# Differential attention in layers 0 and 3: six tiles of queries and keys by Strassen's scheme

## The reference, cut to what matters

```python
def diff_attention(h, w_in, lam, subln_g, w_out, rel_bias, lam_init):
    q, k, v = jnp.split(h @ w_in, 3, axis=-1)
    q = q.reshape(B, S, DA_HEADS, 2, HEAD_DIM)
    k = k.reshape(B, S, DA_HEADS, 2, HEAD_DIM)
    v = v.reshape(B, S, DA_HEADS, 2 * HEAD_DIM)
    ...
        s = jnp.einsum('bqhcd,bkhcd->bhcqk', qb, k).astype(jnp.float32) * scale + bias[None]
        pr = masked_softmax(s, mask)
        a = pr[:, :, 0] - lam_full * pr[:, :, 1]
        return jnp.einsum('bhqk,bkhe->bqhe', a.astype(v.dtype), v)
    ...
    o = rmsnorm(o, subln_g) * (1.0 - lam_init)
    return o.reshape(B, S, D_MODEL) @ w_out
```

## Time and profile before

| | us |
|---|---|
| median of 3 runs | 2436.51 (2435.25 to 2438.89) |
| the profiled execution | 2434.99 |
| its span in the trace | 2433.0 |

### The profile page before, as it was taken

How to read it: one execution, slowest core, us unless ns; L and a number is a source line. 1 busy time by engine, 2 the same in 40 slices (tenths; PEclk the granted TensorE clock), 3 DMA queues, 4 the chain that set the end, 5 groups by cost and what they waited for, 6 DMA issues and landing times.

```text
span 2433.0 us, 31769 instructions
## 1 busy us (share of the span) xinstructions
PE 2338.7 (96%) x12496; PEld 1549.0 (64%) x12496; DVE 1033.6 (42%) x2557; ACT 562.3 (23%) x1350; POOL 89.4 (4%) x125
## 2 busy tenths in 40 slices
PE   7999999999999999999999999999999989999997
PEld 5689648768945777964787974767433348743333
DVE  1447764455676333766532867623200017220001
ACT  2333003342301322210323320223111122311111
POOL 1000000000000000000000000100000000000000
PEclk9999999999999999999999999999999999999999
DMA  9435754413765332666432575642999995289996
GB/s 364 184 139 213 282 197 173 148 61 130 265 255 208 130 121 104 237 248 242 152 125 104 200 279 212 234 176 90 384 377 387 393 357 198 100 350 421 394 393 260
DMA packets 67347, 564.97 MB, mean 232 GB/s; under 512 B 7162, under 2 KB 9523, under 8 KB 19587
## 3 DMA queue, kind: packets, MB, share of 16 engines
q1 hardware_dynamic: 47232, 470.60, 50.4%
q0 software_dynamic: 15696, 83.24, 8.9%
q10 hardware_dynamic: 4274, 9.12, 1.0%
HBM read 688.72 MB, written 26.45 MB: 294 GB/s over the span
## 4 chain that ended last, share of the span: by engine, by line
PE 64%; DMA 8%; DVE 3%; ACT 2%; issue 1%; POOL 0%; SPq 0%; POOLq 0%; ACTq 0%; DVEq 0%
PE work L501 51%; PE acc L501 12%; DMA weight_ring<-in_stream 5%; DMA expert_rows<-oT 1%; PE work L555 1%; DMA bias<-in_stream 1%; DVE oT L2185 1%; PE acc L555 1%; DMA big<-expert_rows,row_index 0%; DMA token_rows<-big,token_slot 0%; DMA hT<-token_rows 0%; DVE xT L2220 0%; ACT big L1655 0%; SPq L3050 0%; DVE big L2198 0%
## 5 line engine op out<-in xcount | busy, mean ns | idle before, releaser
L501 PE MATMUL work<-hT,weight_ring 128*128 128x256 f32 (+1 forms) x1984 | 387.0, 354 | 3.5 <-DVE stat_max L2371 2.5
L501 PEld LDWEIGHTS work<-hT,weight_ring 128*128 128x128 f32 x1984 | 338.5, 191 | 45.4 <-issue 6.3
L501 PE MATMUL work<-weight_ring,big 128*64 128x512 f32 (+2 forms) x1344 | 293.3, 585 | 12.4 <-DMA weight_ring<-in_stream 7.1
L501 PE MATMUL work<-oT,weight_ring 128*128 128x256 f32 (+1 forms) x1280 | 245.5, 349 | 0.0
L501 PEld LDWEIGHTS work<-oT,weight_ring 128*128 128x128 f32 x1280 | 214.1, 191 | 24.3 <-issue 2.0
L2937 DVE TENSOR_TENSOR big<-work,big 128x512 f32<-128x512 f32 x16 | 11.1, 692 | 472.5 <-PE work L501 472.5
L501 PEld LDWEIGHTS work<-weight_ring,big 128*64 128x64 f32 (+2 forms) x1344 | 89.2, 128 | 179.3 <-issue 176.9
L501 PE MATMUL work<-weight_ring,att 128*32 128x512 f32 (+2 forms) x640 | 174.1, 597 | 4.1 <-ACT att L1655 4.1
L1655 ACT ACTIVATE big<-work 128x512 f32<-128x512 f32 x121 | 69.4, 596 | 321.8 <-PE work L501 297.2
L501 PE MATMUL work<-hT,att 128*128 128x128 f32 (+1 forms) x960 | 141.2, 296 | 0.0
L501 PE MATMUL work<-weight_ring,hT 128*128 128x512 f32 x288 | 129.8, 602 | 11.8 <-DMA weight_ring<-in_stream 10.7
(11 more groups left out here) (366 smaller groups left out, 3032.7 us busy)
## 6 DMA issues: line engine op xcount, KB each, us to landing
weight_ring<-in_stream SPq DMA_DIRECT2D x120, 2048.0 KB
weight_ring<-in_stream SPq DMA_DIRECT2D x226, 1024.0 KB, 8.4
ada_ring<-in_stream SPq DMA_DIRECT2D x56, 1024.0 KB
bias<-in_stream SPq DMA_DIRECT2D x56, 1024.0 KB
ada_ring<-in_ada_stream POOLq DMA_DIRECT2D x48, 1024.0 KB, 7.3
expert_rows<-oT POOLq DMA_DIRECT2D x20, 512.0 KB, 9.3
hT<-token_rows ACTq DMA_DIRECT2D x18, 512.0 KB
token_rows<-bias POOLq DMA_DIRECT2D x11, 512.0 KB, 12.7
```

Of the source, the lines that this page charges most:

```text
L501: return pe.matmul(o, a, b, start=start, stop=stop, skip_group_check=True)
```

## The change

Six of the eight tiles of queries and keys, f = 2 and 3 in layer 0 and f = 0 to 3 in layer 3, are computed by Strassen's scheme in the variant with seven products (Winograd's sums). The weights of a tile are split in queries and keys and in the first and second half of the 1024 inputs; h is split by halves of inputs and halves of tokens. A product is 2 x 4 matmuls of 128 x 128 (16 records), so a tile has 56 matmuls of 128 columns instead of 32 of 256.

Products 1, 6, 7 and 4 accumulate in one PSUM bank (the chain): ACT copies the bank after product 1 (`act_mixed`) and product 5's bank; DVE adds after product 6 (L2505, then product 7 may start) and after product 7 (L2515, then product 4 may start). Product 2 is added by L2499, product 3 by L2526; then L2527 multiplies the late keys by `rstd` in place, L2529 scales all queries, and L2531 multiplies the chain bank, after product 4, into the early keys, which frees the bank.

GpSimd makes four weight sums per tile, 128x1024 each (L3178), in `ada_ring`, and four input sums per layer, 128x512 each (L3183 to L3188). There is one set of slots: a tile's sums 1, 2, 3, 4 wait until products 5, 6, 7, 3 of the tile before are done. The loads of the adaptive weights come behind them on GpSimd's queue: the first pair behind layer 0's sums, one pair behind layer 3's.

In layer 3 tiles 0 and 1 run their seven products in one go, in the order 1, 5, 6, 2, 7, 3, 4; all others as 2, 1, 5, 6 in one step and 7, 3, 4 in the next. In layer 3 the mean over squares of step 4 moves behind the fill (`late_mean`).

The diff, cut to its core:

```diff
+        def mixed(st):
+            return range(2 if first_da(st) else 0, 4)
+        def together(st, f):
+            return not first_da(st) and f < 2
+        def mixed_order(st, f):
+            return (1, 5, 6, 2, 7, 3, 4) if together(st, f) else (2, 1, 5, 6, 7, 3, 4)
+        def mixed_banks(st, f):
+            parts = units_of(st)[0]
+            chain, third = parts[2 + 2 * f], parts[3 + 2 * f]
+            fifth, second = (chain - 1, chain + 1) if together(st, f) else (chain - 1, chain - 2)
+            return {1: chain, 6: chain, 7: chain, 4: chain, 2: second, 5: fifth, 3: third}
+        def pe_mixed(pe, st, p):
...
+            for at, product in enumerate(order[begins:begins + 4], begins):
+                o, w, data = operands[product]
+                if product in (1, 2, 3, 5):
+                    pe_open(pe, banks[product])
+                if product in (3, 5, 6, 7):
+                    pe.wait_ge(head_weights, 4 * g + {5: 1, 6: 2, 7: 3, 3: 4}[product])
+                if product in (4, 5, 6, 7):
+                    pe.wait_ge(head_inputs, 4 * (st.layer > 0) + {5: 1, 6: 2, 7: 3, 4: 4}[product])
+                if product == 6:
+                    pe.wait_ge(chain_kept, g + 1)
+                elif product in (7, 4):
+                    pe.wait_ge(chain_added, 2 * g + (1 if product == 7 else 2))
+                for m in range(2):
+                    for k in range(4):
+                        ins = mm(pe, o[:, m * P:m * P + P], w[:, k, m * P:m * P + P], data[:, k],
+                                 (m, k) == (0, 0) and product in (1, 2, 3, 5), k == 3)
...
                 for p in fill_of(st)[s]:
-                    pe_part(pe, st, p, parts[p])
+                    if is_mixed(st, p):
+                        pe_mixed(pe, st, p)
+                    else:
+                        pe_part(pe, st, p, parts[p])
+                if late_mean(st, s):
+                    sub_squares(0)
...
+        def act_mixed(act, st, p):
+            wait_mixed(act, st, f, 1)
+            nc.scalar.activation(q_early, wk(banks[1], 0, S).rearrange("p (m t) -> p m t", m=2), ACT.Copy).then_inc(chain_kept, 1)
+            wait_mixed(act, st, f, 5)
+            nc.scalar.activation(k_late, wk(banks[5], 0, S).rearrange("p (m t) -> p m t", m=2),
+                                 ACT.Copy).then_inc(evac[banks[5] % 4], 1)
...
+        def dve_mixed_heads(v, st, p):
+            wait_mixed(v, st, f, 3)
+            v.wait_ge(chain_added, 2 * g + 2)
+            v.tensor_tensor(q[:, :, P:S], third, q[:, :, P:S], ALU.add).then_inc(evac[banks[3] % 4], 1)
+            v.tensor_tensor(k[:, :, P:S], k[:, :, P:S], by(1), ALU.mult)
+            wait_evacuated(v, [banks[2], banks[3]])
+            v.scalar_tensor_tensor(q, q, DH ** -0.5, over_tokens(2), ALU.mult, ALU.mult)
+            wait_mixed(v, st, f, 4)
+            v.tensor_tensor(k[:, :, 0:P], chain, by(0), ALU.mult).then_inc(evac[banks[4] % 4], 1)
...
+        def pool_mixed(pool, st):
+            def weights(f):
+                pool.wait_ge(landed[tile.slot], 16 * tile.turn)
+                for i, product, a, b, op in ((1, 5, w(1, 0), w(1, 1), ALU.add), (2, 6, mixed_weight_sum(1), w(0, 0), ALU.subtract),
+                                             (3, 7, w(0, 0), w(1, 0), ALU.subtract), (4, 3, w(0, 1), mixed_weight_sum(2), ALU.subtract)):
+                    if f > mixed(st)[0]:
+                        wait_mixed(pool, st, f - 1, product)
+                    if i in (2, 4):
+                        pool.wait_ge(head_weights, n + i // 2)
+                    pool.tensor_tensor(mixed_weight_sum(i), a, b, op).then_inc(head_weights, 1)
+            weights(mixed(st)[0])
+            pool.wait_ge(h_ready, 8 * st.at["h"])
+            pool.wait_ge(work_full, units_of(st)[2]["means"] + 1)
...
+            for f in mixed(st)[1:]:
+                weights(f)
+            wait_mixed(pool, st, 3, 3)
...
             copy_rows(pool, rows2, copies2, 0, 8, copies_out[2])
+            first_mixed, second_mixed = [st for st in plan if st.kind == "da"]
+            pool_mixed(pool, first_mixed)
             for a in range(2):
                 pool.dma_start(ada_ring[:, a, :], ada_stream[a]).then_inc(ada_landed[a], 16)
...
                 pool_gate_sums(pool, ple)
+                if ple.layer + 1 == second_mixed.layer:
+                    pool.wait_ge(ada_step, 16 * (end + 1))
+                    pool_mixed(pool, second_mixed)
+                    for a in range(2):
+                        pool.dma_start(ada_ring[:, a, :], ada_stream[2 * end + 2 + a]).then_inc(ada_landed[a], 16)
```

More of the change, by code:

```diff
@@ L620, in nsa_done, with late_mean @@
             return [p[0] if isinstance(p, tuple) else p for p in NSA_FILL.get(s, ()) if not isinstance(p, tuple) or p[1] == 1]
+        def late_mean(st, s):
+            return s == 4 and st.kind == "da" and not first_da(st)
         def units_of(st):
@@ L636, in units_of @@
                 at += 1
+                if kind == "da" and not first_da(st) and p == 2:
+                    parts[p] = at
+                    at += 2
                 if kind == "fox" and p == 1:
@@ L657, in units_of @@
                     at += 2
-                if kind == "da" and s in (4, 6):
+                if kind == "da" and s in (4, 6) and not late_mean(st, s):
                     other[(s - 4) // 2] = at
@@ new lines, in is_mixed, with wait_mixed, mixed_weights @@
+        def is_mixed(st, p):
+            return st.kind == "da" and 2 <= p < 10 and p // 2 - 1 in mixed(st)
+        def wait_mixed(eng, st, f, product):
+            if product in (1, 7, 4):
+                eng.wait_ge(head_products, 3 * mixed_number(st, f) + (1, 7, 4).index(product) + 1)
+            else:
+                eng.wait_ge(work_full, mixed_banks(st, f)[product] + 1)
+        def mixed_weights(st, f, upper, later):
+            whole_tile = slot_of(tiles[st.at["tile"] + 1 + f].slot, 0, TILE).rearrange("p (k c) -> p k c", k=KB)
+            return whole_tile[:, 4 * later:4 * later + 4, upper * S:upper * S + S]
@@ new lines, in mixed_weight_sum, with mixed_input, mixed_input_sum @@
+        def mixed_weight_sum(i):
+            return slot_of(RING, (i - 1) * 1024, 1024).rearrange("p (k c) -> p k c", k=4)
+        def mixed_input(later, late):
+            return hT[:, :].rearrange("p (k c) -> p k c", k=KB)[:, 4 * later:4 * later + 4, late * P:late * P + P]
+        def mixed_input_sum(i):
+            return blk(big, SQ + 2 * (i - 1), 2).rearrange("p (k c) -> p k c", k=4)
+        def pe_mixed(pe, st, p):
+            f, g = p // 2 - 1, mixed_number(st, p // 2 - 1)
+            banks, order, begins = mixed_banks(st, f), mixed_order(st, f), 4 * (p % 2)
+            second, fifth, chain, third = (wk(banks[n], 0, S) for n in (2, 5, 1, 3))
+            weights = lambda upper, later: mixed_weights(st, f, upper, later)
+            operands = {1: (chain, weights(0, 0), mixed_input(0, 0)), 2: (second, weights(0, 1), mixed_input(1, 0)),
+                        3: (third, mixed_weight_sum(4), mixed_input(1, 1)), 4: (chain, weights(1, 1), mixed_input_sum(4)),
+                        5: (fifth, mixed_weight_sum(1), mixed_input_sum(1)), 6: (chain, mixed_weight_sum(2), mixed_input_sum(2)),
+                        7: (chain, mixed_weight_sum(3), mixed_input_sum(3))}
+            if p % 2 == 0:
+                pe_tile(pe, st.at["tile"] + 1 + f)
+            for at, product in enumerate(order[begins:begins + 4], begins):
[14 more added lines that the diff above has]
+                                 (m, k) == (0, 0) and product in (1, 2, 3, 5), k == 3)
+                        if (at, m, k) == (0, 0, 0):
+                            ins.then_inc(tile_begun, 1)
+                ins.then_inc(head_products if product in (1, 7, 4) else work_full, 1)
@@ L743, in pe_da @@
                     pe_pair(pe, turns[n], n, 8 + n)
[L744 to L751, removed]
+                if s >= 4 and s % 2 == 0 and not late_mean(st, s):
+                    sub_squares((s - 4) // 2)
                 if 0 <= s - 1 < 8:
@@ L2393, in dve_da @@
                     v.sem_inc(logits_ready, 1)
+                fill = [p for p in fill_of(st)[s] if p < 10]
+                if len(fill) == 1 and fill[0] % 2 == 1:
+                    dve_mixed_chain(v, st, fill[0])
                 if s < 8:
@@ L3094, in _ @@
             for ple in [st for st in plan if st.kind == "ple"]:
-                with pool.Fori(ADA_PER // 2 * ple.layer, min(ADA_PER // 2 * (ple.layer + 1), n_ada // 2 - 1)) as i:
+                end = ADA_PER // 2 * (ple.layer + 1) - (ple.layer + 1 >= second_mixed.layer)
+                with pool.Fori(ADA_PER // 2 * ple.layer, end) as i:
                     pool.wait_ge(ada_step, i * 16 + 16)
```

95 lines of the change are left out of this document (87 added, 8 removed).

## The result

The changed kernel takes 2444.37 us (median of seven; 2442.7 to 2454.2), the one before 2436.51 beside it; the ratio is 1.0041, 95% interval 1.0024 to 1.0057. It is slower, by about half of what was forecast: +7.9 between the medians, where the 2450.6 of the forecast stood for +14.1, and +8.7 between the profiled executions (2443.66 against 2434.99), where the sum gave +15.6. The profiled execution has a span of 2442.0 us, 9.0 more than before.

The account below looks back on a forecast made before the run. PE, busy for 96% of the span, was taken as the bound. Products -7.9, layer 3 +9.6, layer 0 +6.9 and clock +7.0 gave +15.6 on 2434.99: 2450.6, own range 2441 to 2458, stated range 2431 to 2460.

Parts of the forecast that it names:

- places 1 and 2: Ends of layer 3's first and second tiles: query scaling waits for GpSimd's sum 4, delaying pairs 0 and 2, +2.2 each.
- place 3: Layer 3, step 2: softmax additions wait for sums 3 and 4, so pair 4 starts late, +3.5.
- rival A: DVE's scalings of one input by a column are blocked too; +3.9 at place 3 and layer 0, 2454.5; chance 0.22.
- the signs named: Expected trace marks: sums about 2.4, blocked DVE operations at 2 us and more, PE idle before pairs, clock under 1 behind.
- Layer 0: Step 1's softmax additions and key multiplication wait for sums, pair 3 waits 6.3; fifth product 0.5; in all +6.9.
- Layer 3: Waits ahead of pairs 0, 2 and 4 plus small ones: +9.6 before savings and clock.
- the small ones: Layer 3: second tile's first product waits 0.7, the sixth 0.5, the moved mean 0.5; +1.7 taken.
- The clock's term, 7.0: PE's clock falls behind four new waits over 2 us, 1.75 each as at 61.95; 0 as other end.
- The gate's DVE work: Layer 3's first-tile sums lie beside DVE work of the gate: 0 to 2 us, taken as 0.
- B: No lasting block: DVE slips in at the first gap and GpSimd is held back; 2429.9; chance 0.15.
- C: Shorter blocks, with sums of 1.9 us, and no fall of the clock; 2438.4; chance 0.14.
- D: GpSimd becomes the bound: sums of 4 us or held back by DVE, PE waits at tiles; near 2472; chance 0.04.

Follow-up runs that it names:

- e1: Changed kernel with most weight sums of the four later tiles cut to 8 columns instead of 1024; 2439.27 us, ratio 1.0016 to the kernel before.
- e5: Changed kernel, weight sums 1 and 2 held until DVE finished the previous tile's heads, 3 and 4 also until softmax weights; 2430.38 us, ratio 0.9974.
- e2: Changed kernel with each 128x1024 weight sum issued as four of 128x256; 2442.38 us, ratio 1.0021 to the kernel before.
- e3: Changed kernel with a tile's weight sums held until DVE has finished the heads of the tile before; 2436.89 us, ratio 1.0011 to the kernel before.
- e8: As e5 in layer 3; in layer 0 weight sums 3, 4 and input sums 3, 4 wait for pair 0's softmax weights; 2429.17 us, ratio 0.9972.
- e7: Changed kernel with 12 dummy 128x256 matmuls on PE in the wait ahead of pair 3 in layer 0; 2442.81 us, one run.

## Why the prediction was right, and where its sizes were off

**Right in sign, and in the mechanism at places 1 and 2.** The products save what was worked out. DVE's operations with two SBUF inputs wait for GpSimd's running sum, and the pairs wait for DVE (e1, e5). A sum of 128x1024 takes 2.35 to 2.53 beside these tiles; 2.43 was taken. At place 3 and in layer 0 the pairs waited as forecast, but the operations that stood were in the main others (rival A, below): there the forecast, given 0.45, had the wrong operations, and A, given 0.22, the right ones. Of the signs named, the key multiplication took 0.55 and not 2 us, and the clock fell behind two of the four waits.

**Layer 0** was forecast at -2.6 + 6.9 + 1.75 = +6.05 (6.3 and 0.5 make 6.8, not 6.9) and measured +6.9: 5.73 for the 6.3 of the stall, 0.81 for the 0.5 of the input sum, 2.9 for one fall of the clock. That 6.3 came so near is in part luck: the last sum ended at 81.33 and not at 82.4, and from there to the pair it took 2.8 and not 1.7, since the softmax additions and the addition from a bank stood behind that sum too. After a pause this long the pair and the transposes were slow too, which the row at 61.95, from which the 1.75 came, does not contain.

**Layer 3** was forecast at -5.2 + 9.6 + 5.25 = +9.65 and measured +3.7. This is where the forecast failed in size. The stalls came to +7.5, not 9.6: +1.5 instead of 2.2 at places 1 and 2 (the last sum began 0.8 us after product 3's end and not 1.1; behind it DVE needed 0.54, 0.41 and a hand-over of 0.15, not 0.7, 0.42 and 0.3), +3.3 for 3.5 at place 3, 1.1 for the small ones' 1.7. The small ones themselves came as forecast (0.69 ahead of the second tile's first product, 0.46 at its product 6, 0.52 ahead of the moved mean); what the sum left out is that waits of 0.55 in the kernel before, ahead of that mean and of pair 6, went away.

**The clock's term, 7.0, is the one that was mis-sized.** Windows of the changed kernel (PEclk is the third number from the end) behind the waits of layer 0, place 1 (two windows), place 2 and place 3:

```profile
84.00:86.40 2.40, 2.28 (x11) 1.66 (x12) 0.00 (x0) 0.00 (x0) 0.00 (x0) 0.50 0.00 0
1234.50:1236.70 2.20, 1.56 (x16) 1.15 (x16) 1.20 (x8) 0.02 (x1) 0.00 (x0) 1.00 0.00 0
...
1238.60:1242.00 3.40, 3.25 (x29) 3.09 (x28) 1.68 (x6) 2.35 (x10) 1.29 (x1) 1.00 0.80 323
...
1252.00:1256.00 4.00, 3.75 (x34) 3.45 (x35) 2.21 (x13) 1.52 (x6) 0.00 (x0) 1.00 0.36 78
...
1271.60:1274.00 2.40, 2.35 (x12) 1.73 (x13) 0.00 (x0) 0.00 (x0) 0.00 (x0) 0.50 0.00 0
```

It fell behind 5.73 and 3.51 and not behind 2.38 and 2.37. Its cost in this execution was 2.9, 0, 0 and 1.5, in all 4.4 of 7.0. (The row at 1238.61, 4.12 instead of 3.74, is not the clock, which stands at 1.00 there, but the wait of product 6: in e5 the same two products stand as two rows, the second with 0.15 ended by ACT's L1990.) The row that pointed to this, a wait of 2.52 without a fall, was in the earlier trace rows; I had taken it for the exception.

**Costed at nothing.** The gate's DVE work beside the first tile's sums cost 0.5 (of 0 to 2): two of its operations on SBUF (L2440, L2441) take 1.42 and 2.72 instead of 0.69. The adaptive weights' loads cost nothing that the traces show. Elsewhere the difference changes by itself: the fall at 121.73 of the kernel before is missing in this execution (-1.4), one at 475.87, behind a wait of 2.32, is new (+1.6), and the second block, which waits for transfers, gives back 2 of the 10.9 us at the end of layer 3.

**Rival A was right in its mechanism and wrong in its price.** The scalings are blocked: L2572, on two columns, takes 2.30 where 0.23 is usual.

```profile
64.24 2.30 DVE L2572 TENSOR_SCALAR stat_coef<-stat_coef,lamv 128x2 f32<-128x2 f32 x1
```

The Trainium skill ("SBUF — State Buffer", "Who interferes with whom") names both cases, two SBUF inputs and a scaling that works in a 2-port mode. The traces agree that both are blocked (L2529 2.83 instead of 0.68, L2572 2.30 instead of 0.23). But more blocked operations did not make the stall longer: a blocked operation uses up a sum, and the three sums left in step 1 of layer 0 stretch three operations, whichever come first. The end is set by the last sum, not by the count of operations that could be blocked; that is why 6.3 could hold although it was worked out with the wrong operations.

**The others.** B (no lasting block) and C (sums of 1.9) are refuted by the rows at 1231.16 and 1228.60. D did not come with the change, but did in e2.

## What to carry to other kernels

In these traces work that is moved to GpSimd is not beside DVE but in turn with it, wherever DVE reads two SBUF operands (2.83 instead of 0.68) or scales in SBUF (2.30 instead of 0.23); operations that read PSUM run on (0.42 beside a sum). So place GpSimd's instructions by semaphores in the stretches where DVE reads PSUM or waits, and look at what stands behind a late DVE operation in its order (a bank to be freed), not only at its own reader. Shorter GpSimd instructions help DVE but lengthen GpSimd's own queue (four quarters take 2.76, the whole 2.35).

## What the runs showed of the hardware that was not expected

The clock behind a wait of 1.9 to 2.6 us went either way. It fell behind 1.90 (at 61.64; the 32 records took 5.44 instead of 3.74) and 2.32 (475.87) in the changed kernel, 2.14 and 2.58 in the kernel before, 2.34 (1255.72) in e3 and 2.41 (1272.18) in e2. It did not behind 2.38, 2.37 and 2.58 (128.52) in the changed kernel, 2.27 (470.66) in the kernel before, 1.95 (62.11) in e2 and 2.40 (63.03) in e8. Behind 2.96 (e7), 3.51 and 5.73 it fell; why the shorter ones differ stays open.

A 2-column scaling is stretched as long as one of 128 or 256 columns (L2572 2.30 us, L2542 at most 2.44). A 128x4 reciprocal just ahead of such a scaling, beside the same sum, is not (0.17 at 75.19, ahead of 1.35).

The block goes both ways. GpSimd's sum at 1187.48, which began while a DVE operation over 2048 columns with two SBUF inputs (L2425) still ran (to 1188.21), took 2.94 instead of 2.35.
